# Second layer's input projections as 2x2 block products, by token quarters in three banks

## The chip, the cores and the metric

The kernel runs on one core of one Trainium2 chip. The metric is the device time of one execution in microseconds; before the change it is 1141.55 us, the median of three runs. All arithmetic is float32; the matmuls that matter take their operands as pairs of a rounded value and a residue (below).

## The reference

One step of a two-layer decoder trunk for 1024 prompt tokens and 8 x 4 sample tokens, 1056 columns in all, model width 1024:

```
h = rms_norm(x, norm_pre[i]);  a, b, c, z = split(h @ w_in[i], 4)      # each 1024 wide
layer 0:  u = c * a;  conv = w0*u[t-2] + w1*u[t-1] + w2*u[t];  y = (b * conv * silu(z)) @ w_out[0]
layer 1:  q = silu(a) * 128**-0.5;  f = lb + (1 - lb) * sigmoid(b);  k = 1 - f;  v = c
          S_t = diag(f_t) S_{t-1} + k_t^T v_t;  o_t = q_t S_t         # 8 heads of 128
          y = (rms_norm(o) * silu(z)) @ w_out[1]
x = x + rms_norm(y, norm_post[i])
```

The outputs are x for both kinds of tokens, the last inputs of the convolution, and the states S after the last token.

## The kernel before

Activations lie with features on the 128 partitions and tokens on the free axis. Every float32 matmul is three passes over rounded values and residues: weight high x tokens high, weight low x tokens high, weight high x tokens low. ScalarE writes the high part (a rounding copy), VectorE subtracts it to get the low one (`split_hi`, `split_lo`).

**Layer 1** (the gated convolution) already forms most of its projections as 2x2 block products: two tiles of 128 outputs and the two halves of the tokens, seven products m1 to m7 of half the depth (`PRODUCTS`, L571) for the eight of the plain form. VectorE forms the sums of weight blocks (L1409 to L1418), ScalarE rounds each (L987), VectorE takes residues (L1426); products are summed in four pairs of PSUM banks, moved by ScalarE (L1011) and combined by VectorE (L1470). Each block product runs over both quarters of its half before the next begins.

**Layer 2** projects tile by tile: `group` (L531) has eight depth blocks of three passes, 24 matmuls of 352 columns, for each third of the tokens, in banks 0 to 2. The first three tiles (v, q, f of head 0) run before the loop, in the order `FIRST`. The loop `iteration(j, last)` then projects q of head j, z of head j-1, v and f of head j, and between the twelve groups runs the recurrence `rec(j - 1, s, last)` of the head before, step by step, in banks 3 to 7:

- step 0: the output of head j-2 is turned (L725) and gated by VectorE (`gate`, L1697); step 1: v is turned (L741), the output's high and low parts are written
- step 3: products within chunks (L747), which wait for `vs`, VectorE's last small copy of step 1 (L1728); before it come `prepare` (L1676 to L1691), two reciprocals (L1713, L1714) and six strided products (L1722)
- steps 4, 5, 6, `MID` and 7: levels of 4, 8, 16, 32 and 64 tokens (L712, L717); VectorE scales r_Q and r_K (L1652, L1653) ahead of each next level
- step 8: k is turned (L785); step 9: chunk states (L790), summed one after the other by VectorE (L1783, L1786); step 10: outputs (L797, L799), their squares (ScalarE, L1204), sums (VectorE, L1793), roots (L1206) and scaling (L1801)

q and z leave PSUM as a sigmoid (ScalarE) times the bank itself (VectorE, L1813). After the loop come z of head 7 and the recurrence of head 7, with the first rows of the output product (L644) in its gaps.

Order is by hand: each engine has one list of instructions and waits on event counters that other engines raise. For example, the products of step 3:

```
pe.wait_ge(VR.sem, VR.at(h, "vs"))
for c in range(CK):
    nc.tensor.matmul(bank[3 + c // 4][:, tokens(c % 4)], r_K[:, tokens(c)], r_Q[:, tokens(c)],
                     start=True, stop=True)
```

Between the layers each row block of 128 tokens is normalised, turned (`turned`, L1600) and written to `reg_a` as high and low parts (L1115, L1606). SP issues the loads of weights and rows in one queue, ScalarE's queue those of the states.

## Time and profile before

| | |
|---|---|
| median of three runs | 1141.55 us (1141.32 to 1141.58) |
| the profiled execution, its own time | 1141.34 us |
| its span, first to last instruction | 1139.6 us |
| TensorE matmul busy | 1103.8 us, 97% |
| VectorE busy | 743.7 us, 65% |
| ScalarE busy | 366.7 us, 32% |
| granted clock of TensorE, mean | 0.99 of 2.4 GHz |

The own time holds some work at both ends that the span doesn't. Matmuls are pipelined: the time of one overlaps the next, so the pace of a run of them is read from start to start.

### The profile page before, as it was taken

To read this page: it belongs to the slowest core of one execution; us is meant where nothing else is said; L and a number is where in the kernel's file an instruction comes from. 1 tells how busy PE (TensorE), PEld (TensorE's weight loads), DVE (VectorE), ACT (ScalarE), POOL (GpSimd) and SP (SyncE) were. 2 spreads that over 40 slices of the span, in tenths; PEclk is the share of its full clock that TensorE was granted. 3 is DMA by queue.
4 is the path that set the end of the run, shared out by engine and by line. 5 is a ranking of instruction groups with operands and counts; after the bars stand their busy time and mean duration, and the time that the engine had idled before them with its cause. 6 is when DMAs were issued, how large, how long until landed. Compare 5 with 4: busy or idle time off the path is not lost.

```text
span 1139.6 us, 19775 instructions
## 1 busy us (share of the span) xinstructions
PE 1103.8 (97%) x7721; PEld 1037.9 (91%) x7721; DVE 743.7 (65%) x1279; ACT 366.7 (32%) x694; POOL 28.8 (3%) x36
## 2 busy tenths in 40 slices
PE   5989999999999999999999999999999999978998
PEld 4989999999999888799999999999999999977875
DVE  6798677677678366618486584957659586585155
ACT  6343333333345244422241321323132241322122
POOL 2000000000000000000000010100101010010000
PEclk8999999999999999999999999999999999989999
DMA  6102121121212532121121111111111111111143
GB/s 213 36 20 75 38 75 37 41 69 37 74 37 74 187 111 98 59 57 54 40 59 38 40 55 55 40 55 40 36 58 55 37 58 54 59 56 57 61 150 115
DMA packets 93315, 74.28 MB, mean 65 GB/s; under 512 B 2519, under 2 KB 85528, under 8 KB 93274
## 3 DMA queue, kind: packets, MB, share of 16 engines
q1 hardware_dynamic: 75482, 64.80, 18.2%
q10 hardware_dynamic: 17792, 8.91, 2.7%
q8 instruction: 28, 0.46, 0.2%
q14 instruction: 13, 0.11, 0.0%
HBM read 60.26 MB, written 13.44 MB: 65 GB/s over the span
## 4 chain that ended last, share of the span: by engine, by line
PE 92%; DVE 4%; issue 1%; DMA 1%; ACT 1%; SPq 0%; ACTq 0%; DVEq 0%
PE bank L531 32%; PE bank L571 24%; PE bank L644 17%; PE bank L717 4%; PE bank L551 3%; PE bank L747 2%; PE bank L712 1%; PE bank L765 1%; PE bank L797 1%; PE bank L790 1%; PE bank L799 1%; PE bank L659 1%; PE bank L785 1%; PE bank L725 1%; PE bank L741 1%
## 5 line engine op out<-in xcount | busy, mean ns | idle before, releaser
L531 PE MATMUL bank<-reg_a,wsplit 128*128 128x352 f32 x2304 | 389.9, 326 | 0.6 <-ACT arena L1130 0.6
L531 PEld LDWEIGHTS bank<-reg_a,wsplit 128*128 128x128 f32 x2304 | 368.3, 188 | 4.5 <-issue 2.3
L571 PE MATMUL bank<-reg_a,wsplit 128*128 128x264 f32 x1344 | 165.5, 284 | 1.0 <-DVE o_raw L1456 1.0
L571 PEld LDWEIGHTS bank<-reg_a,wsplit 128*128 128x128 f32 x1344 | 164.0, 188 | 1.2 <-issue 1.2
L571 PE MATMUL bank<-reg_b,w_ring 128*128 128x264 f32 x1008 | 124.7, 284 | 1.2 <-DVE wraw L1412 1.2
L571 PEld LDWEIGHTS bank<-reg_b,w_ring 128*128 128x128 f32 x1008 | 123.3, 188 | 1.4 <-DVE wraw L1412 1.4
L644 PE MATMUL bank<-reg_a,reg_b 128*128 128x512 f32 (+1 forms) x324 | 77.9, 395 | 1.0 <-DVE reg_a L1292 1.0
L644 PE MATMUL bank<-reg_b,reg_a 128*128 128x512 f32 (+1 forms) x324 | 77.1, 395 | 0.0
L644 PEld LDWEIGHTS bank<-reg_a,reg_b 128*128 128x128 f32 (+1 forms) x324 | 57.8, 179 | 18.7 <-DVE reg_a L1292 1.7
L644 PEld LDWEIGHTS bank<-reg_b,reg_a 128*128 128x128 f32 (+1 forms) x324 | 57.8, 179 | 17.0
L1652 DVE TENSOR_TENSOR arena<-arena,r_tt 128x512 f32<-128x512 f32 x40 | 27.6, 691 | 52.5 <-PE bank L717 46.9
L1470 DVE TENSOR_TENSOR arena<-arena,bank 128x264 f32<-128x264 f32 x84 | 35.0, 428 | 34.5 <-PE bank L571 33.3
L987 ACT ACTIVATE w_ring<-wraw 128x512 fp32r<-128x512 f32 x42 | 26.5, 633 | 76.3 <-PE bank L571 76.3
L1575 DVE TENSOR_TENSOR arena<-bank,arena 128x512 f32<-128x512 f32 (+1 forms) x28 | 19.0, 684 | 48.0 <-ACT arena L1092 48.0
L1011 ACT ACTIVATE arena<-bank 128x264 f32<-128x264 f32 x84 | 32.2, 389 | 49.4 <-PE bank L571 44.7
L485 POOL TENSOR_TENSOR kv_stacked<-v_stacked,bmask 96x1024 fp32r<-96x1024 f32 x8 | 22.6, 2831 | 975.3 <-DVE arena L1728 975.3
L717 PEld LDWEIGHTS bank<-arena 128*128 128x128 f32 x384 | 45.5, 192 | 1.3 <-issue 0.4
L1292 DVE TENSOR_TENSOR wsplit<-wraw,wsplit 128x1024 fp32r<-128x1024 f32 x36 | 43.5, 1208 | 4.7 <-ACT wsplit L902 4.7
L717 PE MATMUL bank<-arena 128*128 128x64 f32 x384 | 46.1, 273 | 0.0
L1130 ACT ACTIVATE arena<-bank 128x352 f32<-128x352 f32 x24 | 11.1, 462 | 101.5 <-PE bank L531 101.5
L1128 ACT ACTIVATE arena<-bank 128x352 f32<-128x352 f32 x24 | 11.0, 464 | 93.9 <-PE bank L531 93.9
L987 ACT ACTIVATE wsplit<-wraw 128x512 fp32r<-128x512 f32 x42 | 25.0, 627 | 49.4 <-DMA wraw<-in_w_in 36.5
(217 smaller groups left out, 1479.3 us busy)
## 6 DMA issues: line engine op xcount, KB each, us to landing
wraw<-in_w_in SPq DMA_DIRECT2D x64, 512.0 KB, 4.1
arena<-in_x_prompt SPq DMA_DIRECT2D x16, 512.0 KB, 3.8
wraw<-in_w_out SPq DMA_DIRECT2D x16, 512.0 KB, 3.3
x_scratch<-arena SPq DMA_DIRECT2D x8, 512.0 KB, 2.7
arena<-in_state_hgrn ACTq DMA_DIRECT2D x8, 512.0 KB, 3.9
out<-arena ACTq DMA_DIRECT2D x8, 512.0 KB, 2.9
arena<-x_scratch SPq DMA_DIRECT2D x8, 512.0 KB, 3.3
out<-arena SPq DMA_DIRECT2D x7, 512.0 KB, 2.6
```

The costliest lines, as they stand in the source:

```text
L485: pool.tensor_tensor(kv_stk[0:STK, 0:NB * P].rearrange("p (b v) -> p b v", b=NB), v_stk[0:STK, :].bitcast(F32).unsqueeze(1).broadcast_to([ ...
L531: mm = nc.tensor.matmul(bank[b][:, 0:CH], w[wi][:, k, :], rhs[hi], start=(k == 0 and i == 0), stop=(k == KT - 1 and i == 2))
L551: mm = nc.tensor.matmul(bank[b][:, 0:QT], w[wi][:, k, :], src[hi][:, k % KH, cols], start=(k == 0 and i == 0), stop=(k == KT - 1 and i == 2))
L571: mm = nc.tensor.matmul(bank[banks[q]][:, 0:QT], w[wi][:, k, :], B_OP[name][hi][:, k, q * QT:(q + 1) * QT], start=(start and k == 0 and i ...
L644: mm = nc.tensor.matmul(bank[b][0:r, :], src[side][:, k, i * P:i * P + r], w[wi][:, half * HALF:(half + 1) * HALF], start=(start and side ...
L717: mm = nc.tensor.matmul(b[:, c * 64:(c + 1) * 64].rearrange("p (b r) -> p b r", r=m), r_K[:, tokens(c)], rhs, start=True, stop=True)
L747: nc.tensor.matmul(bank[3 + c // 4][:, tokens(c % 4)], r_K[:, tokens(c)], r_Q[:, tokens(c)], start=True, stop=True)
L987: A(w_block(name)[0], A_RAW[name], ACT.Copy).then_inc(W_HI.now(name), 1)
L1011: A(dst[:, q * QT:(q + 1) * QT], bank[banks[q]][:, 0:QT], ACT.Copy).then_inc(C_ACT.now(f"{what}{s}{q}"), 1)
L1292: V.tensor_tensor(d, wraw[:, s], h.bitcast(F32), ALU.subtract).then_inc(w_lo, 1)
L1470: V.tensor_tensor(dst[:, cols], src[:, cols], bank[banks[q]][:, 0:QT], ALU.add).then_inc(C_DVE.now(f"{what}{s}{q}"), 1)
L1652: V.tensor_tensor(qr, qr, tl.unsqueeze(2).broadcast_to([P, nb, m]), ALU.mult)
```

## The change

All of layer 2's projections but the first three tiles and the last z are made as block products: tiles z of head j-1 and q of head j are one pair, f and v of head j another. Unlike in layer 1, all seven products run for one quarter of the tokens before the next quarter, in three banks whose roles X, Y, Z rotate (`H_BANKS`); the recurrence steps stand after certain products (`REC_AT`). The turned rows are also stored to DRAM and read back by halves for the sums of token blocks, which are written where `reg_b` was; so the heads' outputs go to DRAM (`o_scratch`) and come back for the output product, in the order `O_SEQ`. The last z tile is formed with the operands that exist (`last_z`). silu is one ScalarE function in place of a sigmoid and a multiplication, in layer 1 too; the reciprocals are fewer; q's scaling and the affine of f move to ScalarE; chunk states have a place of their own (`r_sc`). Waiting order within step 5 changes, and the state update of step 7 moves up (`rec 6.25`).

```diff
...
+        def quadrant(kk, tt):
+            return [v[:, kk * KH:(kk + 1) * KH, tt * HT:(tt + 1) * HT] for v in planes(reg_a)]
+        H_OP = {"m1": quadrant(0, 0), "m2": quadrant(1, 0), "m3": quadrant(1, 1), "m6": operand(reg_b, 0),
+                "m7": operand(reg_b, 1), "m5": operand(reg_b, 2), "m4": operand(reg_b, 3)}
...
+        H_BANKS = ((0, 1, 2), (1, 2, 0), (2, 0, 1), (0, 1, 2))
+        REC_AT = {(0, "m2"): 0, (0, "m5"): 1, (1, "m2"): 3, (2, "m1"): 4, (2, "m6"): 5, (2, "m7"): 6, (2, "m4"): MID,
+                  (2, "m3"): 7, (3, "m1"): 8, (3, "m2"): 9, (3, "m7"): 10}
...
+            def store_turned(i):
+                r = rows_of(i)
+                sp.wait_ge(V_TR.sem, V_TR.at(i, "gb"))
+                sp.dma_start(h1_dram[:, :, i * P:i * P + r],
+                             o_tr[i % 2].rearrange("p (k t) -> p k t", k=KT)[:, :, 0:r]).then_inc(h_st[i % 2], 16)
...
+                if i:
+                    store_turned(i - 1)
+                if i == 6:
...
+                    sp.dma_start(T_B11, h1_dram[:, 0:KH, 0:HT]).then_inc(t_in[0], 16)
+                    sp.dma_start(T_B21, h1_dram[:, KH:, 0:HT]).then_inc(t_in[0], 16)
...
+            store_turned(TT - 1)
+            sp.wait_ge(y_done, TT)
+            sp.wait_ge(h_st[0], 80)
+            sp.wait_ge(h_st[1], 64)
+            sp.dma_start(T_B12, h1_dram[:, 0:KH, HT:]).then_inc(t_in[1], 16)
+            sp.dma_start(T_B22, h1_dram[:, KH:, HT:]).then_inc(t_in[2], 16)
...
+            def pair_quarter(j, g, last, first=False):
+                side, q = g // 2, g % 2
+                p = 2 * j - 2 + side
+                X, Y, Z = H_BANKS[g]
+                before = (p, 0) if q else (p - 1, 1)
+                def old_c11():
+                    pe.wait_ge(H_DVE.sem, H_DVE.at(before[0], f"c11{before[1]}"))
+                def old_c21():
+                    pe.wait_ge(H_DVE.sem, H_DVE.at(before[0], f"c21{before[1]}"))
+                def old_x():
+                    pe.wait_ge(H_ACT.sem, H_ACT.at(before[0], f"x{before[1]}"))
+                def product(name, b, start):
+                    if q == 0:
+                        pe.wait_ge(H_LO.sem, H_LO.at(p, name))
+                    w, src = h_block(name), H_OP[name]
...
+                    mm.then_inc(H_PE.now(f"{name}{q}"), 1)
+                    if (g, name) in REC_AT:
+                        rec(j - 1, REC_AT[g, name], last)
+                if g == 0 and first:
+                    for c in range(NCH):
+                        pe.wait_ge(bank_free[c], emptied(bank_use(NW2) + NCH))
+                elif g == 0:
+                    old_x()
+                else:
+                    old_c11()
+                product("m1", X, True)
+                if g == 0 and not first:
+                    old_c11()
+                elif g:
+                    old_c21()
+                product("m2", Y, True)
+                pe.wait_ge(H_ACT.sem, H_ACT.at(p, f"m1{q}"))
+                product("m6", X, False)
+                if g == 0 and not first:
+                    old_c21()
+                elif g:
+                    old_x()
+                product("m7", Z, True)
+                pe.wait_ge(H_ACT.sem, H_ACT.at(p, f"u2{q}"))
+                product("m5", X, False)
+                pe.wait_ge(H_ACT.sem, H_ACT.at(p, f"m7{q}"))
+                product("m4", Z, False)
+                pe.wait_ge(H_ACT.sem, H_ACT.at(p, f"u4{q}"))
+                product("m3", X, False)
...
+            pe.wait_ge(w_lo, NWZ + 1)
+            pe.wait_ge(H_ACT.sem, H_ACT.at(LASTH, "x1"))
+            last_z("a", 0)
+            pe.wait_ge(H_DVE.sem, H_DVE.at(LASTH, "c111"))
+            last_z("b", 0)
+            rec(KT - 1, 0, KT - 2)
+            pe.wait_ge(Z_ACT.sem, Z_ACT.at(0, "a0"))
+            last_z("x", 0)
+            pe.wait_ge(H_DVE.sem, H_DVE.at(LASTH, "c211"))
+            last_z("a", 1)
+            pe.wait_ge(Z_DVE.sem, Z_DVE.at(0, "b0"))
+            last_z("b", 1)
+            rec(KT - 1, 1, KT - 2)
+            pe.wait_ge(Z_ACT.sem, Z_ACT.at(0, "a1"))
+            last_z("x", 1)
...
-                A(o_raw[:, q * QT:(q + 1) * QT], bank[J0_BANK[q]][:, 0:QT], ACT.Sigmoid).then_inc(F_ACT.now(f"g{q}"), 1)
+                A(o_raw[:, q * QT:(q + 1) * QT], bank[J0_BANK[q]][:, 0:QT], ACT.Silu).then_inc(bank_free[q], 1)
...
+                    elif last is not None:
+                        act.wait_ge(o_rdy, last + 1)
+                        act.dma_start(o_dram[bass.ds(last, 1)].rearrange("h p t -> p (h t)"), r_o).then_inc(o_st, 16)
...
+            def token_top(name, event, done=None):
+                act.wait_ge(H_SUM.sem, H_SUM.at(0, event))
+                src = {"m6": T_B22, "m7": T_B12, "m5": T_B11, "m4": T_B21}[name]
+                if name == "m5":
+                    act.wait_ge(H_SUM.sem, H_SUM.at(0, "l7"))
+                if name == "m4":
+                    act.wait_ge(H_SUM.sem, H_SUM.at(0, "l5"))
+                A(H_OP[name][0], src, ACT.Copy).then_inc(H_TOP.now(f"h{name[1]}"), 1)
+            def pair_hi(p, name, first=False):
...
+                else:
+                    act.wait_ge(H_LO.sem, H_LO.at(p, {"m6": "s2", "m7": "s3", "m5": "s1", "m3": "s4"}[name]))
...
+                A(h_block(name)[0], H_RAW[name], ACT.Copy).then_inc(H_HI.now(name), 1)
...
+            def forget(h, q):
+                act.wait_ge(H_DVE.sem, H_DVE.at(2 * h - 1, f"c21{q}"))
+                if q == 0:
+                    act.wait_ge(VR.sem, VR.at(h - 1, "k3"))
+                A(both(r_f, q), both(r_kr, q), ACT.Sigmoid).then_inc(FN.now(f"f{q}"), 1)
+                A(both(r_kr, q), both(r_kr, q), ACT.Sigmoid, scale=-1.0).then_inc(FN.now(f"k{q}"), 1)
+                act.wait_ge(FN.sem, FN.at(h, f"f{q}"))
+                act.wait_ge(lb_set, h + 1)
+                A(both(r_f, q), both(r_f, q), ACT.Identity, bias=lbh[:, 0:1], scale=lbh[:, 1:2]).then_inc(FN.now(f"a{q}"), 1)
+            def scale_q(h, events):
+                act.wait_ge(FN.sem, FN.at(h, "s"))
+                A(r_Q, r_q, ACT.Copy, scale=QSCALE).then_inc(*FN.many(*events))
...
+            scale_q(0, ("Q", "f1", "k1", "a1"))
+            def move(j, g, name, last):
+                side, q = g // 2, g % 2
+                p = 2 * j - 2 + side
+                X, Y, Z = H_BANKS[g]
...
+                act.wait_ge(H_PE.sem, H_PE.at(p, f"{name}{q}"))
+                if name == "m1":
+                    if g == 0:
+                        act.wait_ge(FN.sem, FN.at(j - 1, "Q"))
+                    A(top[:, first_half], bank[X][:, 0:QT], ACT.Copy).then_inc(H_ACT.now(f"m1{q}"), 1)
+                elif name == "m6":
+                    if last is not None or g:
+                        act.wait_ge(H_DVE.sem, H_DVE.at(before[0], f"c21{before[1]}"))
+                    A(mv_u2, bank[X][:, 0:QT], ACT.Copy).then_inc(H_ACT.now(f"u2{q}"), 1)
+                elif name == "m7":
+                    A(mv_m7, bank[Z][:, 0:QT], ACT.Copy).then_inc(H_ACT.now(f"m7{q}"), 1)
+                elif name == "m5":
+                    if g == 0 and last is not None:
+                        act.wait_ge(o_rdy, last + 1)
...
+                    A(low[:, second_half], bank[X][:, 0:QT], ACT.Copy).then_inc(H_ACT.now(f"u4{q}"), 1)
+                else:
+                    A(top[:, second_half], bank[X][:, 0:QT], ACT.Copy).then_inc(H_ACT.now(f"x{q}"), 1)
+            def silus(j):
...
+                A(r_q, r_q, ACT.Silu).then_inc(FN.now("s"), 1)
+                A(r_g, r_g, ACT.Silu).then_inc(FN.now("g"), 1)
+            def iteration(j, last, final=False):
+                for g in range(4):
+                    for name in PRODUCTS:
+                        if name not in ("m2", "m4"):
+                            move(j, g, name, last)
+                        if (g, name) == (0, "m1") and last is not None:
+                            forget(j - 1, 1)
+                        if (g, name) in REC_AT:
+                            rec(j - 1, REC_AT[g, name], last)
+                        if (g, name) == (2, "m5"):
+                            silus(j)
+                        if (g, name) == (3, "m6"):
...
+                            forget(j, 0)
+                            preload(ACT.Sqrt)
+                        if (g, name) == (3, "m5"):
+                            rec(j - 1, 11, last)
+                            scale_q(j, ("Q",))
+                        if g % 2 and not (final and g == 3):
+                            pair_hi(2 * j - 2 + (g + 1) // 2, name)
...
             def prepare(h):
...
-                V.tensor_copy(r_Q, r_q).then_inc(VR.now("qc"), 1)
-                dve.wait_ge(VR.sem, VR.at(h, "lb"))
-                V.tensor_scalar(r_K, r_kr, lbh[:, 1:2], None, ALU.mult).then_inc(VR.now("k"), 1)
-                V.tensor_scalar(r_f, r_f, lbh[:, 1:2], lbh[:, 0:1], ALU.mult, ALU.add).then_inc(VR.now("fa"), 1)
-                dve.wait_ge(VR.sem, VR.at(h, "fa"))
+                dve.wait_ge(FN.sem, FN.at(h, "a1"))
                 V.tensor_scalar(r_f, r_f, F_FLOOR, None, ALU.max).then_inc(VR.now("f"), 1)
                 dve.wait_ge(VR.sem, VR.at(h, "f"))
                 V.tensor_tensor(r_tt[:, :], every(r_f, 2, 0), every(r_f, 2, 1), ALU.mult).then_inc(VR.now("tt"), 1)
+                if h is not 0:
+                    dve.wait_ge(sp_out, h * 16)
+                V.tensor_scalar(r_K, r_kr, lbh[:, 1:2], None, ALU.mult).then_inc(VR.now("k"), 1)
...
-                    V.reciprocal(inv_f, r_f.rearrange("p (b n) -> p b n", n=B4)[:, :, 1:3]).then_inc(VR.now("rf"), 1)
-                    V.reciprocal(inv_t, every(r_tt[:, :], 2, 1)).then_inc(VR.now("rt"), 1)
+                    V.tensor_tensor(one, f1, t1, ALU.mult).then_inc(VR.now("g3"), 1)
+                    dve.wait_ge(VR.sem, VR.at(h, "g3"))
+                    V.reciprocal(one, one).then_inc(VR.now("rr"), 1)
+                    dve.wait_ge(VR.sem, VR.at(h, "rr"))
+                    V.tensor_tensor(two, one, t1, ALU.mult).then_inc(VR.now("i1"), 1)
+                    V.tensor_tensor(three, one, f1, ALU.mult).then_inc(VR.now("it"), 1)
+                    dve.wait_ge(VR.sem, VR.at(h, "it"))
+                    V.tensor_tensor(one, three, f3, ALU.mult).then_inc(VR.now("i2"), 1)
+                elif s == 0.5:
+                    dve.wait_ge(FN.sem, FN.at(h, "Q"))
+                    dve.wait_ge(VR.sem, VR.at(h, "i2"))
+                    for ap, i, factor, name in ((r_Q, 0, two, "q0"), (r_Q, 2, f2, "q2"), (r_Q, 3, t1, "q3"),
+                                                (r_K, 0, f1, "k0"), (r_K, 2, one, "k2"), (r_K, 3, three, "k3")):
+                        V.tensor_tensor(every(ap, B4, i), every(ap, B4, i), factor, ALU.mult).then_inc(VR.now(name), 1)
                 elif s == 1:
...
+            lower_bound(0)
+            dve.wait_ge(t_in[0], 32)
+            dve.wait_ge(t_in[1], 16)
+            V.tensor_tensor(T_B11, T_B12, T_B11, ALU.subtract).then_inc(H_SUM.now("t1"), 1)
+            dve.wait_ge(t_in[2], 16)
+            dve.wait_ge(H_SUM.sem, H_SUM.at(0, "t1"))
+            V.tensor_tensor(T_B12, T_B22, T_B12, ALU.subtract).then_inc(H_SUM.now("t3"), 1)
+            V.tensor_tensor(T_B22, T_B22, T_B11, ALU.subtract).then_inc(H_SUM.now("t2"), 1)
             split_lo(NW2 + 3, 0)
...
+            token_low("m6", "h6")
+            dve.wait_ge(H_SUM.sem, H_SUM.at(0, "t2"))
+            V.tensor_tensor(T_B21, T_B21, T_B22, ALU.subtract).then_inc(H_SUM.now("t4"), 1)
+            pair_sum(0, "s1")
+            pair_lo(0, "m1")
+            pair_sum(0, "s2")
+            pair_lo(0, "m2")
+            token_low("m7", "h7")
+            token_low("m5", "h5")
+            token_low("m4", "h4")
+            dve.wait_ge(proj_done, G_IN2 + 9)
+            pair_sum(0, "s3")
+            pair_sum(0, "s4")
+            for name in PRODUCTS[2:]:
+                pair_lo(0, name)
...
+            def add_c11(j, g):
...
+                dve.wait_ge(H_ACT.sem, H_ACT.at(p, f"m1{q}"))
+                dve.wait_ge(H_PE.sem, H_PE.at(p, f"m2{q}"))
+                V.tensor_tensor(top, top, bank[H_BANKS[g][1]][:, 0:QT], ALU.add).then_inc(H_DVE.now(f"c11{q}"), 1)
...
+            def next_pair(p, name):
+                if name == "m1":
+                    pair_sum(p, "s1")
+                    pair_lo(p, "m1")
+                    pair_sum(p, "s2")
+                elif name == "m2":
+                    pair_lo(p, "m2")
+                    pair_sum(p, "s3")
+                    pair_sum(p, "s4")
+                else:
+                    pair_lo(p, name)
+            def iteration(j, last, final=False):
+                h = j - 1
+                if last is None:
                     for c in range(NCH):
...
+                        dve.wait_ge(bank_free[c], emptied(bank_use(NW2) + NCH))
+                prepare(h)
+                for g in range(4):
+                    for name in PRODUCTS:
+                        if name == "m2":
+                            add_c11(j, g)
+                        elif name == "m5":
+                            add_c22(j, g)
+                        elif name == "m4":
+                            add_c21(j, g)
+                        if (g, name) == (0, "m2"):
+                            rec(h, 0, last)
+                        elif (g, name) == (0, "m4"):
+                            rec(h, 0.5, last)
+                        elif (g, name) == (0, "m3"):
+                            rec(h, 1, last)
+                        elif (g, name) == (1, "m6"):
+                            rec(h, 3, last)
+                        elif (g, name) == (2, "m1"):
+                            rec(h, 4, last)
+                        elif (g, name) == (2, "m2"):
+                            lower_bound(j)
+                        elif (g, name) == (2, "m6"):
+                            rec(h, 5, last)
+                        elif (g, name) == (2, "m7"):
+                            rec(h, 6, last)
+                            rec(h, 6.25, last)
+                        elif (g, name) == (2, "m4"):
+                            rec(h, MID, last)
+                        elif (g, name) == (2, "m3"):
+                            rec(h, 7, last)
+                        elif (g, name) == (3, "m6"):
+                            rec(h, 9, last)
+                        elif (g, name) == (3, "m5"):
+                            rec(h, 10, last)
+                        elif (g, name) == (3, "m4"):
+                            rec(h, 11, last)
+                        if final and (g, name) == (3, "m7"):
+                            split_lo(NWZ + 1, 1)
+                        if g % 2 and not (final and g == 3):
+                            next_pair(2 * j - 2 + (g + 1) // 2, name)
```

## Rows read from the trace of the kernel before

**Rows 1.** Windows: stretch, its length, busy us (instructions) of each engine, PE clock, DMA
```profile
127.00:331.00 204.00, 204.00 (x1683) 204.00 (x1682) 145.64 (x276) 70.67 (x140) 0.00 (x0) 1.00 0.18 52
...
583.95:651.63 67.68, 67.68 (x497) 65.82 (x496) 45.96 (x80) 18.80 (x35) 2.97 (x1) 1.00 0.17 49
...
990.00:1007.00 17.00, 10.18 (x62) 9.43 (x59) 15.01 (x19) 2.91 (x6) 2.96 (x1) 0.80 0.09 31
```

**Rows 2.** Timeline of TensorE in the conv loop: start, us, engine line op
```profile
165.42 11.82 PE L571 MATMUL bank<-reg_a,wsplit 128*128 128x264 f32 x96
...
185.82 11.82 PE L571 MATMUL bank<-reg_a,wsplit 128*128 128x264 f32 x96
```

**Rows 3.** Timeline of TensorE in layer 2
```profile
498.50 23.29 PE L531 MATMUL bank<-reg_a,wsplit 128*128 128x352 f32 x144 [0.65 <-ACT arena L1130]
...
583.95 1.04 PE L725 MATMUL bank<-ident,arena 128*128 128x128 f32 x8
...
589.05 1.04 PE L741 MATMUL bank<-ident,arena 128*128 128x128 f32 x8
...
651.63 1.03 PE L725 MATMUL bank<-ident,arena 128*128 128x128 f32 x8
...
1003.08 3.78 PE L747 MATMUL bank<-arena 128*128 128x128 f32 x16 [6.82 <-DVE arena L1728]
```

**Rows 4.** Lines of VectorE by form: count, busy us, mean ns, idle before
```profile
L1292 DVE TENSOR_TENSOR wsplit<-wraw,wsplit 128x1024 fp32r<-128x1024 f32 x36 | 43.5, 1208 | 4.7 <-ACT wsplit L902 4.7
...
L1470 DVE TENSOR_TENSOR arena<-arena,bank 128x264 f32<-128x264 f32 x84 | 35.0, 428 | 34.5 <-PE bank L571 33.3
...
L1426 DVE TENSOR_TENSOR w_ring<-wraw,w_ring 128x512 fp32r<-128x512 f32 x42 | 28.9, 690 | 6.9 <-ACT w_ring L987 6.9
...
L1813 DVE SCALAR_TENSOR_TENSOR arena<-arena,bank 128x352 f32<-128x352 f32 x48 | 24.1, 515 | 19.9 <-ACT arena L1128 10.6 <-ACT arena L1126 9.2
...
L1401 DVE TENSOR_TENSOR reg_b<-o_raw,reg_b 128x2112 fp32r<-128x2112 f32 x2 | 4.7, 2356 | 0.9 <-ACT reg_b L970 0.9
```

**Rows 5.** Timeline of VectorE, layer 2
```profile
486.01 0.49 DVE L1600 TENSOR_TENSOR arena<-bank,cst 128x128 f32<-128x128 f32 x2 [1.02 <-PE bank L659]
...
584.67 0.71 DVE L1691 TENSOR_TENSOR r_tt<-arena 128x528 f32<-128x528 f32 x1
...
585.72 1.56 DVE L1697 SCALAR_TENSOR_TENSOR arena<-bank,cst,arena 128x512 f32<-128x512 f32 x3
...
590.56 1.74 DVE L1714 RECIPROCAL arena<-r_tt 128x264 f32<-128x264 f32 x1
...
595.38 1.71 DVE L1722 TENSOR_TENSOR arena<-arena 128x264 f32<-128x264 f32 x3
...
637.35 2.65 DVE L1786 SCALAR_TENSOR_TENSOR arena<-arena,r_tt,bank 128x128 f32<-128x128 f32 x7
...
644.77 1.28 DVE L1793 TENSOR_REDUCE small<-arena 128x4 f32<-128x512 f32 x2 [3.63 <-ACT arena L1204]
```

**Rows 6.** Timeline of ScalarE in the same iteration
```profile
584.24 0.46 ACT L1126 ACTIVATE arena<-bank 128x352 f32<-128x352 f32 x1 [1.82 <-PE bank L531]
...
644.13 1.08 ACT L1204 ACTIVATE arena<-bank 128x512 f32<-128x512 f32 x2 [2.53 <-PE bank L799]
...
645.24 1.28 ACT L1206 ACT_TABLE_LOAD   x1
...
646.53 0.30 ACT L1206 ACTIVATE small<-small,eps 128x8 f32<-128x8 f32 x1
```

**Rows 7.** Lines of ScalarE by form
```profile
L1011 ACT ACTIVATE arena<-bank 128x264 f32<-128x264 f32 x84 | 32.2, 389 | 49.4 <-PE bank L571 44.7 <-DVE arena L1377 4.6
...
L987 ACT ACTIVATE w_ring<-wraw 128x512 fp32r<-128x512 f32 x42 | 26.5, 633 | 76.3 <-PE bank L571 76.3
...
L970 ACT ACTIVATE reg_b<-o_raw 128x2112 fp32r<-128x2112 f32 x2 | 3.9, 1966 | 4.3 <-DVE o_raw L1431 4.3
```

**Rows 8.** DMA issues: KB each, median us from issue to landing
```profile
wraw<-in_w_in SPq DMA_DIRECT2D x64, 512.0 KB, 4.1
```

435 lines of the change are left out of this document (299 added, 136 removed).

## The prediction, on record before the changed kernel ran

> **What bounds the kernel now.** I read the windows by stage first. In the conv loop TensorE is busy 204.00 of 204.00 us, and in one recurrence iteration 67.68 of 67.68, with VectorE at 45.96 and ScalarE at 18.80 [rows 1]. So TensorE's instruction count sets the time in both loops; VectorE has 21.7 us of slack per iteration and ScalarE 48.9. Only at the end of layer 2 does TensorE wait: 6.82 us for VectorE's L1728 (event `vs`) [rows 3]. The reader should keep two numbers: what the change takes from TensorE, and how much of VectorE's 21.7 us it spends.
>
> **What it takes from TensorE.** 168 matmuls of 264 columns (seven block products for one pair of tiles) start 20.40 us apart from the next 168, 121.4 ns each [rows 2]. 144 of 352 columns take 23.29 us with their tail, 161 ns each [rows 3]. An iteration's four tiles are 288 x 0.161 = 46.4 us now and 28 products x 12 x 0.1214 = 40.8 us then; one product is 1.46 us. The recurrence steps keep their matmuls: 67.68 - 46.4 = 21.3 us. Without stalls an iteration would take 62.1 us, 5.6 less. The last z tile costs the same (96 x 0.121 = 11.7 against 72 x 0.161 = 11.6), and the first three tiles stay as they are.
>
> **What it puts on VectorE, per iteration.** Added: 14 residues and 8 weight sums of 512 columns at 0.69 = 15.2, twelve combines at 0.43 = 5.1 [rows 4]. Removed: four residues of a whole tile at 1.21 = 4.8, six evacuations at 0.515 = 3.1 [rows 4], the residue of a head's output 1.2 (1056 columns, as the tile's 1024), the copy of q and one affine, about 0.7 each as a product of r_tt [rows 5]; one reciprocal of 792 columns' worth becomes one of 264 and four products (about 1 less). Net about +9: 55 us. That is 89% of 62.1, and VectorE works strictly in order with waits in between, so it must be walked. ScalarE gets 20 moves at 0.39, 14 roundings at 0.63 [rows 7], silus, and more table loads; it stays near half busy, but its moves are now urgent. With three banks by quarters, X is reused one product after a move is asked for: the move starts 0.29 after the product's end (L725 starts at 583.95, ScalarE at 584.24 [rows 3, 6]) and takes 0.39, about 0.75 with the signal, and 1.46 covers it only if ScalarE has nothing in front.
>
> I walk one iteration in the order of the diff, in us.
>
> *Chain A, from the start of quarter 0 to step 3.* ScalarE's move of m1 ends at 1.46 + 0.29 + 0.39 = 2.15. `forget(j-1, 1)` follows: table load 1.28 [rows 6], two sigmoids of 528 columns and an affine, 0.63 [rows 7] up to 0.75 each, done at 5.35. Only then may VectorE clip: floor, pair product, r_K at about 0.7 each [rows 5], 7.4; combine 0.4; the gate 1.5 [rows 5], 9.3 (that is `o_rdy`); product 0.6, reciprocal 1.74, three products 1.8, two combines 0.8, 14.3; six strided products at 0.57 (three took 1.71 [rows 5]) 3.4, 17.7; two small ones 0.6: `vs` at 18.3. TensorE is there after nine products (13.1), the turn (1.2) and the v transposes (1.0; eight take 1.03 [rows 3]): 15.3. It stalls 2.9, of which about 0.9 already at step 1 for `o_rdy`.
>
> *Chain B, from the end of step 7 to step 10.* VectorE: level 64's two scalings 1.4 (0.69 each [rows 4]), copy and update 0.9, s1 0.6: 2.9. The residue of m1 needs ScalarE's rounding, which stands behind `rec 8`'s two copies (1.08, as in [rows 6]): 4.15. Residue, s2, combine, residue m2, s3, s4: 7.8. Then the eight state updates 0.3 + 2.65 [rows 5]: 10.8. TensorE comes to step 10 after four products (5.8), eight transposes (0.9) and the state products (1.8, about twice eight matmuls): 8.5. Stall 2.3.
>
> *Chain C, from step 10 to the next iteration.* Bank 0 is X of quarter 3 and of the next quarter 0, so the next m1 waits for the move of m3's bank. In front of it on ScalarE, all in order: two squares 1.1, rounding m7, move m5, then the wait for `r1` (VectorE: residue m7, combine, two reductions 1.28 [rows 5]), two roots 0.5 [rows 6], scaled copy of q 1.0, roundings m5 and m4 1.1, the move 0.4. Summed from step 10's end: 7.05; TensorE's m5, m4, m3 end at 4.4. Stall 2.7, where an idle ScalarE would cost 0.75.
>
> *Level 32* now stands behind the three state operations of `rec 6.25` (2.5) and two combines: 0.7 at step 7.
>
> Sum: 62.1 + 2.9 + 2.3 + 2.7 + 0.7 = 70.7, against 67.7: +3.0 each, +21 for seven; the last has no next pair to split, which frees about 2.4 in chains B and C. **Loop: about +19.** Below, the bound is 62.1 + 0.75 (every queue on time); above, each stall also drops the clock: after the idle 6.82 the 16 matmuls of L747 took 3.78, against 2.0 for twice the eight of L741, and the stage's granted clock is 0.80 [rows 1, 3], the lower level, 1.2 GHz for a while: +1.9 a time.
>
> **The hand-over from layer 1.** Token sums need the rows back from DRAM. Nine stores are new on SP; each waits for its row's turn (`gb`), and behind it stand the next row's store of x and load, which wait for still later events, so only the last counts. Its rows are turned at 486.5 [rows 5] and the store of 32 rows takes some 2.4; then come two loads of 1.08 MB. 512 KB land in 4.1 [rows 8]; with half of that fixed, 1.08 MB take 4.3 beyond the fixed part: landed at 495 and 499.5. VectorE: t3 and t2 at 2.35 each [rows 4] after that, 504.3, and only then the residue of the third tile, 505.5: TensorE wanted it at 498.50 + 24 x 0.161 = 502.4 [rows 3], **+3**. Then ScalarE and VectorE take turns with the four operands (1.97 [rows 7] and 2.36), each pair waiting for the other (m5's rounding overwrites m7's raw, m4's m5's), with the evacuations of the f tile between them: the last f bank is free at 523.4, TensorE done with it at 517.1, **+6.2**. ScalarE then rounds five blocks and two long copies ahead of its first move; half a us of that is left at step 3. One fall of the clock, 1.9. Together **+12** (5 if the loads take half as long and the turns overlap; 16 at most, with a second fall).
>
> **The end of layer 2.** It begins one tile before the turn of 583.95 and six iterations on, 580.1 + 6 x 67.7 = 986.3. The z tile comes before step 3 and not around it. b1 shares bank 1 with b0 and waits for `z_low(0)`, behind the reciprocal group: about 13.9 after the start where TensorE is free at 8.4; x1 ends at 19.2, where step 3 started at 16.8 before (1003.08 [rows 3]). Nothing fills TensorE while VectorE does diagonal and factors, and the rounding of w_out's first tile waits for x1: step 4 about 2 to 4 later. Six residues of heads at 1.2 come into a stretch where VectorE already sets the pace, partly in its gaps: +3. **+6** (0 to 12). Heads through DRAM: 0.54 MB out per iteration on ACT's queue and six in, against a DMA share of 0.17 [rows 1]: nothing beside that.
>
> **Silu.** In layer 1 it removes a multiplication of 1056 columns per iteration from VectorE, under a TensorE busy 204 of 204 [rows 1]: 0. If that cover went, 1.2 a time. At most 0.4 is gained before the conv loop, where TensorE waits for the first gate.
>
> **Sum.** 19 + 12 + 6 = +37 to +38 on the profiled 1139.6 us span; that run took 1141.34, 1.74 more, and the median is 1141.55, so I add 38 to the median: **1179.5 us**. A change within 0.2% (2.3 us) can't be told from none.
>
> **A page's rule.** A table load here lasts 1.28 us and the next root starts 0.01 us after its end [rows 6]. The Trainium skill, "ScalarE: Activation LUTs", "What ACT_TABLE_LOAD costs", adds a drain of about 1.38 us to each switch. By it `forget` would end 1.4 later and chain A with it, about 10 us in seven iterations and some 1189 in all; the row speaks against it, so it is a rival with 0.04.
>
> **Rivals.**
> 1. *The queues keep up* (other side). If residues and sums fit in VectorE's gaps and ScalarE's urgent moves are never behind, only 0.75 stays: 7 x (62.85 - 67.7) = -34, with +12 and +6: -16, **1125.5**. For it: VectorE idles 21.7 us an iteration now and the loads add only 9. Against: the three chains are series of dependent instructions whose lengths come from rows. It decides from the point where stalls are under 2.9 us an iteration. 0.18.
> 2. *Only chain C stays*: VectorE is early at `vs` and s7. 7 x (62.1 + 2.7 - 67.7) = -20, +18: **1139.5**. 0.10.
> 3. *The stalls also lower the clock*, 1.9 once an iteration: +13, **1192**. For it: 6.82 idle did it [rows 3]; against: stalls here are under 3. 0.12.
> 4. The drain, above: **1189**. 0.04.
> The walk as it stands: 0.56, own range 1160 to 1195.
>
> Faster: rival 1, half of rival 2, and 0.03 of the walk's lower tail, 0.26. Same 0.05. Slower 0.69. The range reaches from rival 1 less 3 to rival 3 plus 5: 1122 to 1197.
>
> **What would show it.** Projection matmuls of 264 columns at 121 ns, 2448 of them, and an iteration of about 70.7; TensorE idle 2 to 3 us before the 128x128 products of step 3 (released by VectorE's small copy), before step 10 (by the eighth state update), and before the first product of each iteration (by ScalarE's move); VectorE busy 55 an iteration; TensorE idle some 9 us between 502 and 524 with a fall of the clock. Wrong if iterations take under 65 us, if the move of m3's bank starts 0.3 after its product, or if the token blocks land well before 495.

## The result, and the profile of the changed kernel

The changed kernel takes 1184.84 us (median of four runs, 1183.18 to 1189.24) against 1141.57 for the kernel before beside it: 1.0384 times as long, 95% interval [1.0371, 1.0398]. The forecast was 1179.5 with a range of 1122 to 1197. The profiled execution has a span of 1182.4 us, 42.8 more than the 1139.6 of before.

The page of the changed kernel, its span and its busy times by engine:

```profile
span 1182.4 us, 21433 instructions
PE 1090.1 (92%) x8081; PEld 1021.4 (86%) x8081; DVE 813.6 (69%) x1448; ACT 479.4 (41%) x893; POOL 24.8 (2%) x36
```

TensorE, which had no idle time in a recurrence iteration before [rows 1], is now idle in each one. The windows of the changed kernel, one for each of the first three iterations of layer 2, one for the other four, and one for the end (stretch, length, then busy us and instructions of TensorE, its weight loads, VectorE, ScalarE and GpSimd, then the granted clock, the DMA share and GB/s):

```profile
522.42:596.44 74.02, 66.69 (x534) 64.66 (x535) 55.57 (x101) 33.18 (x64) 2.39 (x1) 0.93 0.16 44
596.44:668.49 72.05, 64.81 (x543) 62.58 (x544) 54.12 (x104) 32.10 (x62) 2.40 (x1) 0.98 0.19 53
668.49:739.21 70.72, 64.52 (x543) 62.50 (x544) 54.13 (x104) 32.09 (x62) 2.40 (x1) 0.98 0.19 53
739.21:1021.53 282.32, 257.49 (x2172) 248.78 (x2173) 213.68 (x410) 125.87 (x239) 9.59 (x4) 0.98 0.21 63
1021.53:1182.40 160.87, 140.10 (x744) 113.77 (x744) 86.89 (x145) 47.16 (x93) 1.89 (x1) 0.97 0.26 91
```

Read it in three steps. The first product starts at 522.42, 8.5 us after the loop's start of before (513.9: 96 matmuls of 0.161 after 498.50 [rows 3]). The seven iterations take 499.1 us for 472.2, 26.9 more. The end takes 160.9 for 153.5 (from 986.1, 24 matmuls before the turn at 990.0), 7.4 more. That is the 42.8. In one iteration (668.49) the length less TensorE's busy time, 70.72 - 64.52, is 6.20 us idle; and the granted clock is 0.98, where it was 1.00 [rows 1]. VectorE is busy 54.1 us.

What TensorE waits for in the changed kernel (engine, its line, the line that ends the wait: us in all, times, longest):

```profile
PE bank L943 <- ACT arena L1509: 16.0, 6, 2.7
PE bank L915 <- DVE arena L2122: 12.3, 7, 2.0
PE bank L865 <- DVE arena L2065: 8.5, 6, 1.6
...
PE bank L837 <- DVE arena L2079: 4.9, 1, 4.9
PE bank L1026 <- DVE arena L2296: 4.9, 1, 4.9
PE bank L943 <- ACT arena L1316: 4.4, 1, 4.4
...
PE bank L859 <- DVE arena L2026: 2.9, 4, 0.8
PE bank L943 <- ACT arena L1493: 2.4, 1, 2.4
```

The first three are chains C, B and A of the forecast, in that order. L1509 is the move of m3's bank, L2122 the state updates, L2065 the small copy that sets `vs`. The timeline of TensorE in the iteration from 596.44 on, only instructions behind idle time and the next iteration's start; time start, duration, and in brackets the idle time with what ended it:

```profile
596.44 3.19 PE L943 MATMUL bank<-reg_a,wsplit 128*128 128x264 f32 x24 [2.51 <-ACT arena L1509]
...
606.02 1.09 PE L859 MATMUL bank<-ident,arena 128*128 128x128 f32 x8 [0.75 <-DVE arena L2026]
...
614.59 2.05 PE L865 MATMUL bank<-arena 128*128 128x128 f32 x16 [1.52 <-DVE arena L2065]
...
644.35 1.15 PE L832 MATMUL bank<-arena 128*64 128x64 f32 x16 [0.23 <-DVE arena L1978]
...
656.21 1.22 PE L915 MATMUL bank<-arena 128*128 128x128 f32 x4 [2.02 <-DVE arena L2122]
...
668.49 4.60 PE L943 MATMUL bank<-reg_a,wsplit 128*128 128x264 f32 x24 [2.71 <-ACT arena L1509]
```

The same 24 matmuls take 3.19 us at 596.44 and 4.60 at 668.49, and the first four of step 10 take 1.22 for 0.71 elsewhere: behind some of these gaps the clock is at its lower level (1.2 GHz) for a while. ScalarE ahead of the gap at 668.49 in the changed kernel, its timeline:

```profile
665.35 0.30 ACT L1397 ACTIVATE small<-small,eps 128x8 f32<-128x8 f32 x1 [2.01 <-DVE small L2129]
...
665.95 1.08 ACT L1446 ACTIVATE arena<-arena 128x1056 f32<-128x1056 f32 x1
666.94 1.13 ACT L1426 ACTIVATE reg_a<-wraw 128x512 fp32r<-128x512 f32 x2
667.98 0.37 ACT L1509 ACTIVATE arena<-bank 128x264 f32<-128x264 f32 x1
...
670.58 0.39 ACT L1493 ACTIVATE arena<-bank 128x264 f32<-128x264 f32 x1 [1.72 <-PE bank L943]
670.99 1.28 ACT L1437 ACT_TABLE_LOAD   x1
672.28 0.65 ACT L1437 ACTIVATE arena<-arena 128x528 f32<-128x528 f32 x1
```

TensorE ends m3 at about 665.8. From there on the bank could be moved, but roots, the scaled copy of q (L1446) and two roundings (L1426) stand in front: the move starts at 667.98. That is chain C, and none of these four is needed by the move.

### The profile page after: what moved, and what is told of

Read it like the earlier page. It is cut to its first block, busy times and chain, and to the rows that moved or that the text cites. A ratio compares the mean times of both kernels' runs of the same rounds, so it can differ in the third digit from the quotient of the medians.

```text
span 1182.4 us, 21433 instructions
## 1 busy us (share of the span) xinstructions
PE 1090.1 (92%) x8081; PEld 1021.4 (86%) x8081; DVE 813.6 (69%) x1448; ACT 479.4 (41%) x893; POOL 24.8 (2%) x36
## 4 chain that ended last, share of the span: by engine, by line
issue 88%; PE 9%; DVE 2%; POOL 1%; ACT 0%; DVEq 0%; POOLq 0%; ACTq 0%
PE bank L764 8%; PE bank L837 0%; DVE reg_b L2034 0%; DVE reg_a L1621 0%; POOL kv_stacked L605 0%; DVE arena L2079 0%; ACT reg_b L1353 0%; PE bank L881 0%; PE bank L915 0%; PE bank L908 0%; PE bank L917 0%; DVE arena L1977 0%; DVE arena L2070 0%; DVE arena L1978 0%; DVE arena L2107 0%
## 5 line engine op out<-in xcount | busy, mean ns | idle before, releaser
L691 PE MATMUL bank<-reg_a,wsplit 128*128 128x264 f32 x1344 | 165.5, 284 | 0.6 <-ACT o_raw L1186 0.6
L691 PEld LDWEIGHTS bank<-reg_a,wsplit 128*128 128x128 f32 x1344 | 164.0, 188 | 0.8 <-issue 0.8
L943 PE MATMUL bank<-reg_a,wsplit 128*128 128x264 f32 x672 | 95.8, 298 | 20.4 <-ACT arena L1509 16.0
L943 PEld LDWEIGHTS bank<-reg_a,wsplit 128*128 128x128 f32 x672 | 88.6, 197 | 22.4 <-DVE reg_a L2171 17.2
L943 PE MATMUL bank<-reg_b,wsplit 128*128 128x264 f32 x672 | 91.6, 292 | 2.4 <-ACT arena L1493 2.4
L943 PEld LDWEIGHTS bank<-reg_b,wsplit 128*128 128x128 f32 x672 | 85.2, 192 | 4.6 <-ACT arena L1493 2.6
L943 PE MATMUL bank<-reg_b,reg_a 128*128 128x264 f32 x672 | 88.6, 286 | 0.0
L943 PEld LDWEIGHTS bank<-reg_b,reg_a 128*128 128x128 f32 x672 | 84.3, 189 | 0.6
L2171 DVE TENSOR_TENSOR wsplit<-wraw,wsplit 128x512 fp32r<-128x512 f32 x42 | 40.7, 970 | 23.7 <-ACT wsplit L1426 23.7
```

Of the source, the lines that this page charges most:

```text
L691: mm = nc.tensor.matmul(bank[banks[q]][:, 0:QT], w[wi][:, k, :], B_OP[name][hi][:, k, q * QT:(q + 1) * QT], start=(start and k == 0 and i ...
L943: mm = nc.tensor.matmul(bank[b][:, 0:QT], w[wi][:, k, :], src[hi][:, k, q * QT:(q + 1) * QT], start=(start and k == 0 and i == 0), stop=(k ...
L2171: V.tensor_tensor(lo, H_RAW[name], hi.bitcast(F32), ALU.subtract).then_inc(H_LO.now(name), 1)
```

## The experiments

All but `b_silu` are edits of the changed kernel (1184.84), and each result stands beside the kernel before, 1141.8 to 1141.9 in the three sets. No kernel leaves work out; `e_warm` and `e_best` add idle-time transposes.

**One chain at a time.** Three edits reorder one queue each and change no instruction. The lines below give the orders in short and are not the code.

```diff
 e_x_first, ScalarE, quarter 3:
-  (3, m5): rec 11; scale_q; pair_hi m5    (3, m4): pair_hi m4    (3, m3): move x; pair_hi m3
+  (3, m5): pair_hi m5; rec 11                                    (3, m3): move x; scale_q; pair_hi m4, m3
 e_states_first, VectorE:
-  (3, m2): add_c11; pair_lo m2; sums s3, s4    (3, m6): rec 9
+  (3, m2): add_c11; rec 9; pair_lo m2; sums s3, s4
 e_forget_first, ScalarE, j > 1:
-  (0, m1): move m1; forget(j-1, 1)
+  (0, m1): forget(j-1, 1); move m1
```

> The changed kernel (1184.8 us) with one edit on ScalarE: near the end of an iteration the scaled copy of q and the rounding of m4's block stand behind the move of m3's bank, not in front of it. Theory of the walk (chain C is a queue on ScalarE): the move starts about 1.6 to 1.9 us earlier, the wait before the first product of the next iteration goes from 2.7 us to 0.9 or less, and six of these give 10 to 13 us; with the clock fall behind that wait gone too it may be 10 more: 1162 to 1175. Rival (VectorE's work sets the pace of an iteration, and time taken out here comes back at the next wait for VectorE): under 3 us, 1182 to 1186, with the waits before step 3 or step 10 longer by what was taken out.

Measured: 1169.29 (1166.99 to 1171.05), ratio to before 1.0232 [1.0214, 1.025]: 15.5 us faster. The wait fell from 16.0 to 4.0:

```profile
PE bank L943 <- ACT arena L1509: 4.0, 6, 0.7
```

> The changed kernel with one edit on VectorE: in quarter 3 the eight state updates come straight after the combine behind m2, ahead of the residue of m2's block and of two weight sums. Theory (chain B is a queue on VectorE): the updates start 1.8 us earlier (653.18 against 651.4 in the traced iteration), the wait before step 10 goes from 2.0 us to about 0.3, six of these give 10 us, and with the lower clock behind that wait gone up to 20: 1165 to 1175. Rival (what TensorE gains here it loses at the first product of the next iteration, since ScalarE's queue in chain C is late by its own work): 1183 to 1186, with that wait 1.8 longer.

Measured: 1176.11 (1173.0 to 1180.2), 1.0296 [1.0266, 1.0327]: 8.7 us faster. The wait before step 10 fell from 12.3 to 1.5, but chain C took back 3.5 of it (16.0 to 19.5), as the rival said in part, and five of its six longer gaps (3.02 to 3.31 us) came with the lower clock; the one of 3.30 at 804.22 did not, its 24 matmuls took 3.19:

```profile
PE bank L943 <- ACT arena L1509: 19.5, 6, 3.3
...
PE bank L915 <- DVE arena L2122: 1.5, 7, 0.2
```

> The changed kernel with one edit on ScalarE: at the start of an iteration the table load, the two sigmoids and the affine of the forget gate come ahead of the move of m1, not behind it. Theory (chain A begins with these four): VectorE's clip starts about 2 us earlier, and the wait before the 128x128 products of step 3 (1.24 us in the traced iteration) and the one at step 1 go; the move of m1 is then done about 4 us after the product's start, where m6 wants it at 4 to 5.7: 7 to 11 us in all, 1174 to 1178. Rival (VectorE is held by its own chain of floor, gate and reciprocal, or m6 now waits for the move): 1183 to 1187, with a new wait before m6 that ScalarE's move of m1 ends.

Measured: 1175.54 (1171.5 to 1176.22), 1.0285 [1.0263, 1.0307]: 9.3 us faster. L865's wait fell from 8.5 to 2.6 and the one at step 1 from 2.9 to under 0.6; nothing new stands before m6.

Each chain is real, and VectorE's 54 us an iteration are no floor at this pace: the rivals that said so are out.

**The clock.** Transposes of the identity into unused columns of bank 7 fill part of two of the gaps (`keep_busy(n)` issues n of them):

```diff
                 elif s == 10:
+                    keep_busy(10)
                     pe.wait_ge(VR.sem, VR.at(h, f"s{CK - 1}"))
...
                 elif g == 0:
+                    keep_busy(14)
                     old_x()
```

> The changed kernel with transposes of the identity into unused columns of bank 7: ten ahead of TensorE's wait before step 10 and fourteen ahead of its wait before the first product of an iteration, so that it idles less there (about 0.8 and 1.0 us for 2.0 and 2.7) and does no other work. Theory (the idle time before these points lowers the granted clock, 24 matmuls of 264 columns take 4.60 us for 3.15 and the first matmuls of step 10 start 0.43 us apart for 0.22): 1.5 to 3 us an iteration come back, the time falls by 10 to 20 to some 1165 to 1175, and the granted clock's mean rises. Rival (the clock falls for another reason, or the waits only end later): no change, 1183 to 1187.

Measured: 1178.27 (1176.63 to 1178.51), 1.0318 [1.0301, 1.0335]: 6.6 us faster with 24 instructions more an iteration; less than the 10 to 20 expected, but the sign is the theory's. The window of one iteration of `e_warm`, its granted clock in the third column from the end:

```profile
592.85:663.31 70.46, 65.86 (x568) 63.57 (x568) 54.10 (x104) 32.12 (x62) 2.40 (x1) 1.00 0.19 55
```

The first 24 matmuls now take 3.20 and 3.19 us in the iterations at 592.85 and 663.31, behind 0.98 and 1.17 idle. So the idle time brings the lower clock. It does not do so each time: in the traces of the changed kernel, `e_forget_first`, `e_handover` and `e_end`, 24 gaps of 2.49 to 2.72 us stand in front of an iteration, and 12 of them were followed by it (2.71, 4.60 us for the 24; 2.50 in `e_handover`, 4.44) and 12 not (2.51, 3.19; 2.49 in `e_forget_first`, 3.19). No gap up to 1.3 us in front of an iteration was.

**Together.** `e_three` has the three edits above at once. `e_order2` orders the queues anew (again in short):

```diff
 ScalarE, quarter 3:
-  (3, m5): rec 11; scale_q; pair_hi m5    (3, m4): pair_hi m4    (3, m3): move x; pair_hi m3
+  (3, m5): pair_hi m5; rec 11; scale_q    (3, m4): pair_hi m4    (3, m3): move x
-  (0, m1) of the next: move m1; forget
+  (0, m1) of the next: forget; move m1; pair_hi m3 of the pair before
 VectorE, quarter 3:
-  (3, m2): add_c11; pair_lo m2; s3, s4    (3, m6): rec 9    (3, m7): pair_lo m7    (3, m5): add_c22; rec 10
+  (3, m2): add_c11; rec 9; pair_lo m2; s3, s4               (3, m7): rec 10; pair_lo m7    (3, m5): add_c22
```

m3's residue moves behind the first combine of the next iteration with its rounding.

> The changed kernel with the three orders of the runs before it together: m4's rounding and the scaled copy of q behind the move of m3's bank, the state updates ahead of m2's residue, the forget gate ahead of the move of m1. Theory (three separate chains, each with its own wait): the gains add, 15.5 + 8.7 + 9.3, 1151. Rival with its place: the work put behind the move of m3's bank (2.2 us) and the forget gate (3.2 us) now both stand ahead of the move of m1, which m6 wants about 4.1 us after the iteration's start and which would end at 5.8: a new wait of 1.6 us six times, 1161, shown before the 13th projection matmul after the turn. Second rival (VectorE's 55 us an iteration are the floor under it): over 1165.

Measured: 1159.84 (1155.63 to 1160.44), 1.0147 [1.0126, 1.0167]. The gains don't add (33.5), 25.0 are left, and the rival's new wait is where it was placed, before m6 by the move of m1. Timeline of TensorE in `e_three`:

```profile
658.15 3.19 PE L943 MATMUL bank<-reg_a,wsplit 128*128 128x264 f32 x24 [1.25 <-ACT arena L1509]
...
663.63 3.19 PE L943 MATMUL bank<-reg_b,wsplit 128*128 128x264 f32 x24 [1.24 <-ACT arena L1493]
```

> The changed kernel with the three chains untied and ScalarE's queue put so that nothing stands ahead of a move when its product ends: VectorE makes the squares' two sums before m7's residue, the state updates before m2's residue; ScalarE rounds m5 before the roots, and m3's block only after the forget gate and the move of m1. Theory (the queues' order is what the change loses by, the counted 62.1 us of TensorE's own work is what it wins by): iterations of 63 to 64.5 us for 70.85, no wait above 1 us in them and no fall of the clock: 1184.8 - 6 x 6.9 = 1143, between 1133 and 1150, so about the kernel before. Rival (VectorE's total is too much for the new pace): iterations over 67 us, 1160 or more, with waits for VectorE at step 3 or 10 of 1 us or longer.

Measured: 1148.42 (1147.87 to 1149.11), 1.0058 [1.0041, 1.0075]: 36.4 us faster than the changed kernel. Window of one iteration of `e_order2`, and what is left of its waits on TensorE's timeline:

```profile
590.34:655.46 65.12, 63.03 (x544) 61.01 (x544) 54.04 (x105) 31.65 (x62) 2.40 (x1) 1.00 0.20 59
```

```profile
636.49 1.15 PE L832 MATMUL bank<-arena 128*64 128x64 f32 x16 [0.23 <-DVE arena L1980]
...
646.54 0.71 PE L915 MATMUL bank<-arena 128*128 128x128 f32 x4 [0.21 <-DVE arena L2124]
...
655.46 3.19 PE L943 MATMUL bank<-reg_a,wsplit 128*128 128x264 f32 x24 [0.93 <-ACT arena L1509]
...
671.85 2.05 PE L865 MATMUL bank<-arena 128*128 128x128 f32 x16 [0.72 <-DVE arena L2067]
```

TensorE's own work is 63.0 us, the clock is 1.00, 2.1 us of waits are left, and an iteration takes 2.6 us less than before (67.68 [rows 1]). It is a little above the 63 to 64.5 expected. What the kernel still has over before is in the hand-over and the end: 7.8 us at the loop's start, 13.2 less in the loop (459.0 for 472.2) and 13.0 more in the end. Against the changed kernel the loop alone is 40.1 us shorter (459.0 for 499.1), and 5.6 of that are lost again in the end, whose idle time is the same within 0.3 us and whose clock is lower, 0.91 for 0.97. The window of the end in `e_order2`:

```profile
980.69:1147.20 166.51, 145.46 (x744) 118.39 (x744) 87.90 (x146) 47.28 (x93) 1.89 (x1) 0.91 0.30 104
```

**The hand-over and the end.**

```diff
 e_handover, before the loop:
  VectorE   -  t1; t3; t2; residue of the third tile          +  t1; t3; residue; t2      (and s3, s4, pair_lo m6 ahead of l4)
  ScalarE   -  f bank 1; tokens m4; f bank 2; blocks; affine of f; scaled q; move m1
            +  scaled q while idle; f bank 1; tokens m5; f bank 2; block m6; tokens m4; blocks; affine of f; move m1
 e_end, after the loop:
  ScalarE   -  z_sum(0); forget(7, 1)                         +  forget(7, 1); z_sum(0)
  VectorE   -  gate(6); reciprocal group; z_low(0)            +  gate(6); z_low(0); reciprocal group
```

> The changed kernel with another order at the hand-over alone: the third tile's residue before the sum of t2, the scaled copy of the first q while ScalarE is idle, the last f bank's evacuation ahead of m4's long rounding, m6's block split ahead of m4's tokens. Theory (TensorE waits there for queues, 1.9, 4.4 and 2.4 us): the first two waits shrink by 1.9 and 2.9, the first iteration's chain of VectorE starts about 2 us earlier: 2 to 5 us in all, 1180 to 1183. Rival (VectorE works through its own long token sums and residues without a gap, so the first iteration's step 3 comes when it came before, 542.6): under 1 us.

Measured: 1184.25 (1182.89 to 1185.85), 1.0376 [1.0359, 1.0393], no difference from 1184.84 that counts. Yet step 3 of the first iteration starts at 538.35 for 542.62, 4.3 us earlier, and the end of layer 2 starts 4.3 us earlier too, at 1017.18 for 1021.53. What was won is kept through the loop and gone in the end, which takes 164.4 us for 160.9 with as much idle time (20.8) and a lower clock, 0.93 for 0.97. The window of the end in `e_handover`:

```profile
1017.18:1181.60 164.42, 143.63 (x744) 116.91 (x744) 86.86 (x145) 47.18 (x93) 1.90 (x1) 0.93 0.26 89
```

TensorE's timeline in the loop of `e_handover`:

```profile
590.54 4.44 PE L943 MATMUL bank<-reg_a,wsplit 128*128 128x264 f32 x24 [2.50 <-ACT arena L1512]
...
662.26 5.64 PE L943 MATMUL bank<-reg_a,wsplit 128*128 128x264 f32 x24 [2.66 <-ACT arena L1512]
```

Its iterations from 590.54 and 662.26 take 71.72 and 71.73 us, with the lower clock for up to all of the first 24 matmuls (5.64 for 3.19). That costs little against the changed kernel, whose clock falls in other places: the six iterations after the first take 426.6 us for 425.1. The expectation's rival was right on the total and wrong on the reason. Why the end ran at the lower clock more often is open; each kernel has one profiled execution.

> The changed kernel with another order at the end of layer 2 alone: the last forget gate ahead of the move of z's first part on ScalarE, and VectorE adds z's first part straight after the gate of head 6 and ahead of the reciprocal group. Theory (the last z tile is late for two queues' sake): the wait of TensorE before b1 goes from 4.9 to about 1, x1 ends some 4 us earlier, w_out's first tile with it, and step 4's wait of 4.9 shrinks: 2 to 4 us in all, 1181 to 1183. Rival (VectorE's own work sets the end of layer 2): under 1 us.

Measured: 1181.27 (1180.43 to 1182.85), 1.035 [1.0333, 1.0367]: 3.6 us faster. The wait before b1 is gone, step 4's is 4.18 for 4.87, and 1.83 stands before step 3 now.

> All orders together, without any extra instruction: those of e_order2 in the loop, of e_handover at the hand-over, of e_end at the end of layer 2. Theory (the hand-over's 4 us were won at step 3 of the first iteration, 538.35 for 542.62, and then lost again to the clock of a loop with waits of 2.7 us, which this loop has no more): 1148.4 - 4 - 3 = 1141, between 1138 and 1145. Rival (the hand-over and the end give nothing here either): 1147 to 1149.

Measured: 1136.51 (1135.31 to 1138.28), 0.995 [0.9933, 0.9966]: 5.3 us faster than the kernel before and 11.9 than `e_order2`, where the two edits alone gave 0.6 and 3.6. That is 1.5 below the expected range of 1138 to 1145, and the reason that the expectation gives for the hand-over's 4 us, lost in the loop, does not hold. TensorE's timeline in `e_all`: the loop starts, its second iteration, the end starts.

```profile
518.42 5.62 PE L943 MATMUL bank<-reg_a,wsplit 128*128 128x264 f32 x24 [4.80 <-ACT arena L1316]
...
586.72 3.21 PE L943 MATMUL bank<-reg_a,wsplit 128*128 128x264 f32 x24 [0.84 <-ACT arena L1512]
...
976.99 3.17 PE L1026 MATMUL bank<-reg_a,wsplit 128*128 128x264 f32 x24 [0.57 <-ACT arena L1512]
```

Against the profile of before that is +4.5 at the hand-over (518.42 for 513.9), -13.6 in the loop (458.6 for 472.2) and +6.0 at the end (159.5 for 153.5), together -3.1 of span. Against the profile of `e_order2` it is -3.3 at the loop's start, -0.5 in the loop and -7.0 at the end, of which 2.7 are idle time and 4.3 are a higher clock (0.95 for 0.91). So the gain of the hand-over is there in both loops, with gaps and without; what `e_handover` lost and `e_all` did not is clock in the end.

```diff
 e_best, TensorE, first product m1 of the loop and the wait before its m6:
+                    keep_busy(28)
                     for c in range(NCH):
                         pe.wait_ge(bank_free[c], emptied(bank_use(NW2) + NCH))
...
+                    keep_busy(14)
                 pe.wait_ge(H_ACT.sem, H_ACT.at(p, f"m1{q}"))
```

> As e_all, with 28 transposes of the identity ahead of TensorE's first wait at the hand-over (4.8 us idle) and 14 ahead of the next (2.4 us), which go into unused columns of bank 7. Theory (the idle time lowers the clock: 24 matmuls after each of the two waits took 4.6 and 4.5 us for 3.15): 2 to 3 us under e_all, about 1138, which would be under the kernel before. Rival (the last ones of the extra transposes only end the wait later, or VectorE's chain sets step 3 of the first iteration anyway): no different from e_all.

Measured: 1138.0 (1135.43 to 1141.32, ten runs), 0.9969 [0.9957, 0.9981]. The profile shows what it bought: the first 24 matmuls of the loop take 3.17 us for 5.62, but the next wait grows from 1.43 to 2.37 and step 3 starts at 538.11 for 538.00. Step 3 there waits 1.01 us for VectorE, in `e_all` 1.02: VectorE's chain sets it. No gain, as the rival said.

**Silu alone.** In the kernel before (operands cut):

```diff
-  A(o_raw[...], c_gate[...], ACT.Sigmoid)          # ScalarE, layer 1
-  V.tensor_tensor(own, own, c_gate, ALU.mult)      # VectorE
+  A(o_raw[...], c_gate[...], ACT.Silu)
```

> The kernel before with one part of the change alone: in layer 1 silu is one function on ScalarE, and VectorE's multiplication of 1056 columns an iteration is gone. Theory (under a TensorE that is busy all through the conv loop it is worth nothing): within 0.4 us of the kernel before. Rival (VectorE's queue is on the path there): 1.2 us for each of seven iterations, 8 us faster.

Measured: 1141.94 (1141.18 to 1145.79, ten runs) beside 1141.78: 1.0011 [0.9999, 1.0022]. Window of the conv loop in `b_silu`:

```profile
127.00:331.00 204.00, 204.00 (x1683) 204.00 (x1682) 139.37 (x271) 71.04 (x141) 0.00 (x0) 1.00 0.18 52
```

VectorE is busy 6.3 us less than in [rows 1], TensorE 204.00 of 204.00 as before: nothing.

**GpSimd beside VectorE.** One residue of 128x512 took 2.38 us in every iteration of the changed kernel. `e_pool` is `e_order2` with GpSimd's product later:

```diff
-                pool.wait_ge(VR.sem, VR.at(h, "vs"))
+                pool.wait_ge(VR.sem, VR.at(h, "as"))
```

> As e_order2, but GpSimd's product of 96 x 1024 elements waits for the masked diagonal of the 32 sample rows (event as) and not for vs, so that it runs some 7 us later, beside other work of VectorE. Theory (the residue of 128x512 takes 2.38 us for 0.69 because GpSimd's operation runs meanwhile): the residue is back at 0.69 and the two operations of VectorE with the factors of the pairs, 2.40 us for two, or the one that meets GpSimd's product there, take about 1.7 us longer, one operation held until GpSimd's is done. Rival (that residue is slow for its own sake): it still takes 2.38. The time is no question here: within 3 us of e_order2.

Measured: 1149.13 (1146.84 to 1151.43, two runs), the time of `e_order2`. The timeline of VectorE in `e_order2`:

```profile
606.70 0.69 DVE L2157 TENSOR_TENSOR wraw<-wraw 128x512 f32<-128x512 f32 x1
607.31 2.38 DVE L2173 TENSOR_TENSOR wsplit<-wraw,wsplit 128x512 fp32r<-128x512 f32 x1
```

and of GpSimd there:

```profile
606.75 2.40 POOL L605 TENSOR_TENSOR kv_stacked<-v_stacked,bmask 96x1024 fp32r<-96x1024 f32 x1 [62.70 <-DVE arena L2067]
```

The timeline of VectorE in `e_pool`:

```profile
609.64 0.69 DVE L2173 TENSOR_TENSOR wsplit<-wraw,wsplit 128x512 fp32r<-128x512 f32 x1
...
614.41 2.40 DVE L2081 TENSOR_TENSOR arena<-arena,r_tt 128x1056 f32<-128x1056 f32 x2
616.85 2.02 DVE L2085 TENSOR_TENSOR r_tt<-r_tt 128x264 f32<-128x264 f32 x1
```

and of GpSimd there:

```profile
614.56 4.01 POOL L605 TENSOR_TENSOR kv_stacked<-v_stacked,bmask 96x1024 fp32r<-96x1024 f32 x1 [61.11 <-DVE r_as L2076]
```

The residue is back at 0.69, and the operation that meets GpSimd's now is a product of 264 columns that took 0.43 in `e_order2` and takes 2.02 here, until just after GpSimd's end at 618.57. GpSimd's own takes 4.01 for 2.40. The kernel before has a third case, VectorE and then GpSimd:

```profile
597.75 1.26 DVE L1702 TENSOR_TENSOR reg_b<-arena,reg_b 128x1056 f32 x1
598.93 0.94 DVE L1813 SCALAR_TENSOR_TENSOR arena<-arena,bank 128x352 f32<-128x352 f32 x2
```

```profile
597.80 2.97 POOL L485 TENSOR_TENSOR kv_stacked<-v_stacked,bmask 96x1024 fp32r<-96x1024 f32 x1 [66.10 <-DVE arena L1728]
```

## Why the prediction was right, point by point

**TensorE's own work.** 62.1 us forecast, 63.0 measured (`e_order2`): right within 1.5%.

**Chain A.** `vs` was put at 18.3 after the iteration's start; in the changed kernel the copy ends at 686.57 + 0.28 = 686.85, 18.4 after 668.49. The stall was put at 2.9, 0.9 of it at step 1; it is 0.75 + 1.52 = 2.3 in the iteration at 596.44, since TensorE's own way there takes 15.9, not 15.3. `e_forget_first` takes most of it away: 2.6 us are left of 8.5 at step 3, and under 0.6 of 2.9 at step 1.

**Chain B.** 2.3 forecast, 2.02 measured, and `e_states_first` shows the cause.

**Chain C.** 2.7 forecast, 2.5 to 2.7 measured; `e_x_first` leaves 0.7, where the forecast's idle ScalarE had 0.75.

**Level 32.** 0.7 forecast, 0.23 measured: too much.

**The clock.** Left out of the walk's iteration and given 0.12 as rival 3, at 1.9 an iteration. It is mostly true: in the five iterations from 596.44 to 954.03 TensorE is busy 64.7 us for 63.0 at full clock, 1.7 us an iteration. The forecast's argument against it (the stalls are under 3 us) was wrong.

**The iteration.** 70.7 forecast; those five take 71.5 each. The forecast had 1.8 too much stall (8.6 for 6.8), 0.9 too little work and 1.7 too little for the clock: the sum is better than its terms, and that is luck. The last iteration takes 67.5, where the forecast had 68.3.

**The hand-over.** +12 forecast. Measured: the loop starts 8.5 us late and its first iteration is 3.7 us longer than the five after it, if one counts that it has no head to turn (74.0 for 71.5 - 1.2), about 12 in all. The terms are off here too: the residue comes 1.89 late for 3, the f bank 4.39 for 6.2, the first move 2.43 for 0.5 (two long copies and five roundings stood ahead of it). The clock fell three times and not once, 1.9: behind the 1.89 idle 72 matmuls of 352 columns take 13.35 us for 11.80, and behind the next two waits 24 of 264 columns take 4.70 and 4.72 for 3.2. Against that, step 3 of the first iteration waits for nothing (542.62). The loads' landing was read well: t1 starts at 496.14 and t3 at 498.86, against 495 and 499.5, though the last 128 KB took 4.1 us to DRAM and not 2.4.

**The end.** +6 forecast, +7.4 measured, with both waits in the places named (b1 4.87, step 4 4.87).

**The total.** 19 + 12 + 6 = 37 forecast, 42.8 of span measured: 7.4 at the end, about 12 at the hand-over and about 23 in the loop. So what the forecast was short of is almost all in the loop, 0.8 us in each full iteration, where it had left out the clock's 1.7.

**Silu.** 0 forecast, 0 measured.

**The rivals.** Rival 1 (the queues keep up) and rival 2 (only chain C stays) are out for the changed kernel, since all three chains wait. `e_order2` is rival 1 made by hand: 36.4 us faster, where the forecast's step from the walk to rival 1 was 54: the waits never fall to 0.75 (2.1), the own work is 63.0, and 5.6 us go in the end at its lower clock. Rival 4, a drain behind each table load, is out: the load at 670.99 ends at 672.27 and the sigmoid starts at 672.28, as in [rows 6].

Open: why a gap of 2.5 us is followed by the lower clock in one place and not in another, and why the end of layer 2 ran at 0.97 in some traces and at 0.91 in others. And the end still takes 6.0 us more than before in `e_all`, 2.3 of it idle and 3.7 busy, with 5.52 us of waiting before step 4; which of the work moved there it is for was not tried.

## What to carry to other kernels

A change that takes work from the engine that sets the pace and spreads it over queues that others wait on is worth what its order is worth: here the same instructions took 1184.8 or 1136.5 us. Walk each queue from the instruction that someone waits for backwards and ask of each one in front whether it must be there; then do the walk again for the queue that receives it, as two moves that are right alone can meet (`e_three`). And follow a gain stage by stage before you say where it went: the hand-over's 4 us were still there after the whole loop and went in the end, where the same instructions ran at another clock.

## What the runs showed of the hardware

TensorE's lower clock comes after shorter idle times than the 6.82 us of [rows 3]: once behind a gap of 1.89 us (at the hand-over of the changed kernel), behind some of 2.0 us, behind 12 of 24 gaps of 2.5 to 2.7 us, behind five of six of 3.0 to 3.3 us, and behind 4.8 us in `e_all`; the 24 matmuls after one take 4.4 to 5.6 us for 3.2. The length of the gap alone does not decide it: one of 3.30 us was not followed by it. It also makes stages with the same instructions differ from trace to trace: the end of layer 2 took 160.9 us at 0.97, 164.4 at 0.93 and 166.5 at 0.91, with 20.8 to 21.1 us of idle time in each.

GpSimd and VectorE hold each other up, one operation at a time. GpSimd's product takes 1.89 us where VectorE is idle (at 1040.47 in the changed kernel). In the three cases above it starts beside an operation of VectorE on two operands in SBUF and ends 1.76 us after VectorE is done with it: 609.15 after 607.39, 600.77 after 599.01, and 618.57 after 616.81, where two such operations of VectorE went ahead of it. VectorE's next operation on two such operands then ends 0.3 to 0.5 us after GpSimd's: one went from 0.69 to 2.38 us, another from 0.43 to 2.02. In the kernel before the next one reads a PSUM bank, and it keeps its usual time (0.94 for two, 0.515 for one [rows 4]). Why in `e_pool` the second of two went ahead as well stays open. The Trainium skill, "GPSIMD Engine Reference", "Specifications", lists its SBUF interfaces as shared with VectorE, with contention for VectorE instructions that have two SBUF inputs; these cases agree with it.
